# Expert sums of two prompt tiles as one dense pass over all rows of peer_v, in a fused decoder layer on one core

## The reference

```python
def peer(xn, w):                       # for each token
    ...
    s1 = jnp.einsum("thd,kd->thk", q[:, :, 0], w["peer_keys1"])     # 8 heads, 128 keys
    s2 = jnp.einsum("thd,kd->thk", q[:, :, 1], w["peer_keys2"])
    v1, i1 = lax.top_k(s1, PEER_TOPK)                               # 16
    v2, i2 = lax.top_k(s2, PEER_TOPK)
    ...
    top_s, sel = lax.top_k(cand, PEER_TOPK)                         # 16 of 256 pairs
    e = jnp.take_along_axis(cidx, sel, -1)                          # expert = 128 * key1 + key2
    gate = jax.nn.softmax(top_s.astype(F32), -1)
    act = jax.nn.gelu(jnp.einsum("td,thkd->thk", xb, w["peer_u"][e]).astype(F32), approximate=False)
    coef = (gate * act).astype(xb.dtype)
    return jnp.einsum("thk,thkd->td", coef, w["peer_v"][e])

h = h + peer(rmsnorm(h, w["norm_ffn"]), w)
gate = jax.nn.sigmoid((rmsnorm(h, w["norm_ple"]) @ w["w_ple_gate"]))
return h + gate * (p_i @ w["w_ple_proj"])
```

## Time and profile before

| | us |
|---|---|
| median of 3 runs | 4337.45 |
| lowest, highest | 4336.12, 4348.39 |
| span of the profiled execution | 4331.6 |
| TensorE busy (52%) | 2254.9 |
| VectorE busy (76%) | 3288.1 |
| ScalarE busy (12%) | 522.0 |
| GpSimd busy (51%) | 2201.2 |

### The profile page before, as it was taken

One profiled execution on the slowest core, in us unless ns is written; L12 is line 12 of the kernel. 1 busy time (PEld: TensorE's weight loads), 2 busy tenths in 40 slices (PEclk: granted clock), 3 DMA queues, 4 the chain that ended last, 5 costly groups with the idle time before them and its releaser, 6 DMA issues.

```text
span 4331.6 us, 24058 instructions
## 1 busy us (share of the span) xinstructions
PE 2254.9 (52%) x8238; PEld 1342.1 (31%) x8238; DVE 3288.1 (76%) x3700; ACT 522.0 (12%) x1098; POOL 2201.2 (51%) x1216
## 2 busy tenths in 40 slices
PE   8999815425899492779942457710000920000755
PEld 4456403213475131367731222710000410000322
DVE  0130699997667998868889856699999699988673
ACT  2220112122002001212212010000001000001001
POOL 0000365744332556468775653345667368877441
PEclk9999956657999796767865678955555965555877
DMA  8658789988997999989999899988989999999996
GB/s 294 250 223 287 303 357 364 422 323 335 424 423 299 422 424 414 353 356 365 406 374 360 347 400 413 405 345 339 399 365 405 424 415 422 422 407 422 424 408 234
DMA packets 261153, 1599.51 MB, mean 369 GB/s; under 512 B 27763, under 2 KB 49459, under 8 KB 91750
## 3 DMA queue, kind: packets, MB, share of 16 engines
q0 software_dynamic: 176064, 1268.30, 72.0%
q1 hardware_dynamic: 83078, 320.64, 19.5%
q10 hardware_dynamic: 1888, 9.03, 0.5%
HBM read 1554.75 MB, written 42.56 MB: 369 GB/s over the span
## 4 chain that ended last, share of the span: by engine, by line
PE 31%; DVE 30%; POOL 16%; DMA 13%; issue 7%; ACT 2%; SPq 0%; DVEq 0%; ACTq 0%; POOLq 0%
POOL ring L2549 16%; PE bank L826 14%; DVE ring L1968 11%; DVE total L1993 9%; DMA ring<-in_peer_v,idx_all 5%; DMA ring<-in_peer_u,idx_all 5%; PE bank L1251 4%; PE bank L1288 3%; PE bank L929 1%; PE bank L891 1%; PE bank L800 1%; PE bank L1079 1%; DMA front<-in_cache_kv_latent,page_rows 1%; DVE front L1744 1%; PE bank L1093 1%
## 5 line engine op out<-in xcount | busy, mean ns | idle before, releaser
L1993 DVE SCALAR_TENSOR_TENSOR total<-ring,gate_all,total 128x2048 f32<-128x2048 f32 x571 | 1341.8, 2350 | 188.0 <-DMA ring<-in_peer_v,idx_all 164.5
L2549 POOL DMA_INDIRECT ring<-in_peer_u,idx_all x576 | 1062.2, 1844 | 795.7 <-DVE total L1993 359.1
L2549 POOL DMA_INDIRECT ring<-in_peer_v,idx_all x576 | 1072.2, 1861 | 711.9 <-DVE total L1993 376.3
L1968 DVE CUSTOM_DVE_ANT_0 ring<-ring,xrow 128x2048 f32<-128x2048 f32 x576 | 1297.5, 2287 | 169.4 <-DMA ring<-in_peer_u,idx_all 167.5
L826 PE MATMUL bank<-front 128*128 128x512 f32 (+3 forms) x1920 | 838.3, 594 | 68.9 <-ACT front L2115 64.6
L800 PE MATMUL bank<-inv_diag,front 128*128 128x128 f32 (+1 forms) x304 | 61.9, 391 | 1159.3 <-DVE inv_diag L1378 1102.2
L826 PEld LDWEIGHTS bank<-front 128*128 128x128 f32 (+1 forms) x1920 | 338.4, 181 | 558.5 <-issue 554.5
L800 PEld LDWEIGHTS bank<-inv_diag,front 128*128 128x128 f32 (+1 forms) x304 | 58.9, 299 | 1164.2 <-DVE inv_diag L1378 1098.2
L1251 PE MATMUL bank<-front 128*128 128x128 f32 (+2 forms) x1536 | 257.0, 329 | 20.5 <-DMA front<-in_peer_w_q 17.4
L1251 PEld LDWEIGHTS bank<-front 128*128 128x128 f32 x1536 | 239.8, 192 | 39.3 <-DMA front<-in_peer_w_q 20.3
L2574 POOL DMA_DIRECT2D ring<-in_w_in x12 | 10.7, 894 | 342.8 <-PE bank L1288 239.6
(11 more groups left out here) (323 smaller groups left out, 2894.0 us busy)
## 6 DMA issues: line engine op xcount, KB each, us to landing
front<-in_w_in SPq DMA_DIRECT2D x64, 980.0 KB, 8.4
front<-in_w_out SPq DMA_DIRECT2D x48, 1024.0 KB, 9.1
front<-in_peer_w_q SPq DMA_DIRECT2D x48, 1024.0 KB, 13.3
front<-in_w_ple_gate SPq DMA_DIRECT2D x48, 1024.0 KB, 9.1
ring<-in_w_in POOLq DMA_DIRECT2D x12, 1960.0 KB, 10.5
front<-in_w_uq SPq DMA_DIRECT2D x6, 1536.0 KB, 10.7
ring<-in_peer_u,idx_all POOLq DMA_INDIRECT x576, 14.3
ring<-in_peer_v,idx_all POOLq DMA_INDIRECT x576, 16.0
```

The source lines that it names most:

```text
L1968: e.tensor_tensor_reduce(out=ring[:, b, :], in0=ring[:, b, :], in1=xrow[:, t % 2, :], scale=1.0, scalar=0.0, op0=ALU.mult, op1=ALU.add, ac ...
L1993: e.scalar_tensor_tensor(out=total, in0=ring[:, b, :], scalar=c1, in1=total, op0=ALU.mult, op1=ALU.add).then_inc(s("summed"), 1)
L2549: e.indirect_dma_start(out=ring[:, k % RING, :], out_offset=None, in_=a[("peer_u", "peer_v")[side]][0], in_offset=bass.IndirectOffsetOnAxi ...
```

## The change

Tiles 0, 1 and the sample (`SUMMED`) keep their sums. For tiles 2 and 3 (`DENSE`) only the dots are gathered. When a tile's gates are final, VectorE splits each pick's expert number into key 1 and key 2 (`spread`), TensorE turns both and the gates, and for each token VectorE makes two one-hot rows of 128x128, one with the gate in it; TensorE's product of the two is the token's 128 x 128 matrix of coefficients. ScalarE copies these into a stage and stores them to `c_dram` (16 MB for both tiles). When tile 3 is done too, the coefficients come back in the order of key 1, and TensorE multiplies, for each of 128 slabs of `peer_v` (all its rows, in order) and both tiles, 128x128 coefficients by 128x512 of the slab, 4 banks a tile: 1,024 products that add up in all 8 banks of PSUM. The sums are added to the residual rows, and the second embedding follows. The slots are 896 instead of 1,152.

```diff
+DENSE, SUMMED = [2, 3], [0, 1, 4]
+EB = 8
+GROUP = 4
+CHUNK = 16
...
 # VectorE
+            def spread(j):
+
+                t = DENSE[j]
...
+                e.wait_ge(s("gates_ready"), j + 1)
+                if j == 0:
+                    e.wait_ge(s("slabs_used"), PASSES["dense"])
+                mark(e.tensor_single_scalar(picks_u[:, j, 0, :], idx_all[:, row_units(t)], 7, ALU.logical_shift_right))
+                link(e.tensor_single_scalar(picks_u[:, j, 1, :], idx_all[:, row_units(t)], NKEY - 1, ALU.bitwise_and))
+                e.tensor_copy(picks[:, j, :, :], picks_u[:, j, :, :]).then_inc(s("picks_spread"), 1)
...
+                for q in range(G_GROUPS):
+                    n = j * G_GROUPS + q
+                    yield
+                    if n >= 2:
+                        e.wait_ge(s("g_psum"), n - 1)
+                    for i in range(GROUP):
+                        k = GROUP * q + i
+                        e.tensor_scalar(onehot[:, n % 2, 0, i, :], iota[:, :], picksT[:, j, 0, k:k + 1], picksT[:, j, 2, k:k + 1],
+                                        ALU.is_equal, ALU.mult)
+                        ins = e.tensor_scalar(onehot[:, n % 2, 1, i, :], iota[:, :], picksT[:, j, 1, k:k + 1], None, ALU.is_equal)
+                    ins.then_inc(s("picks_spread"), 1)
...
 # ScalarE
+                    if at == 0 and c >= 2:
+                        e.wait_ge(s(f"c_stored{c % 2}"), 16 * (c // 2))
+                    e.copy(stage[c % 2][:, :, at:at + GROUP].rearrange("p i n -> p n i"),
+                           bank[4 + n % 2][:, :].rearrange("p (n i) -> p n i", n=GROUP)).then_inc(s("g_staged"), 1)
+                    if at == CHUNK - GROUP:
+                        e.wait_ge(s("g_staged"), n + 1)
+                        e.dma_start(c_dram[c], stage[c % 2]).then_inc(s(f"c_stored{c % 2}"), 16)
...
+            def turned_coefficients():
+
+                half = EB // 2
+                for m in range(NKEY // half):
+                    b, i = m // 2, m % 2 * half
+                    yield
+                    e.wait_ge(s("pair_landed0"), 16 * (H_GLA // 2 + b + 1))
+                    if b:
+                        e.wait_ge(s("slabs_used"), PASSES["dense"] + EB * (b - 1) + i + half)
+                    e.copy(CT[:, i:i + half, :, :], CB[:, :, i:i + half, :].rearrange("p c i n -> p i c n")).then_inc(s("coefs_turned"), 1)
...
 # SyncE
+            embedding_loads(0)
+            expert_rows(0, 2)
+            coefficients(0)
+            expert_rows(2, SLABS + 2)
+            for b in range(1, NKEY // EB):
+                coefficients(b)
+                expert_rows(EB * (b - 1) + SLABS + 2, EB * b + SLABS + 2)
+            expert_rows(NKEY - EB + SLABS + 2, NKEY)
...
 # TensorE
+            def expert_sums():
+
+                e.wait_ge(s("g_staged"), G_GROUPS * len(DENSE))
+                for i in range(NKEY):
+                    n = PASSES["dense"] + i
+                    e.wait_ge(s(f"w_landed{n % SLABS}"), slab_landed(n))
+                    if i % (EB // 2) == 0:
+                        e.wait_ge(s("coefs_turned"), i // (EB // 2) + 1)
+                    for sl in range(len(DENSE)):
+                        cols = CT[:, i % EB, sl * P // CHUNK:(sl + 1) * P // CHUNK, :].rearrange("p c n -> p (c n)")
+                        for c in range(4):
+                            mm = e.matmul(bank[4 * sl + c][:, :], cols, W[:, n % SLABS, c * BANK:(c + 1) * BANK],
+                                          start=(i == 0), stop=(i == NKEY - 1))
+                    mm.then_inc(s("slabs_used"), 1)
+                e.wait_ge(s("v_added"), 4 * len(DENSE))
...
-PAGES_BEFORE = [395, 395, 395, 402, 404, 414, 414, 426, 428, 440, 440, 451, 452, 462, 467, 476]
+PAGES_BEFORE = [
+    267, 267, 267, 274, 274, 291, 291, 298, 298, 304, 304, 311, 311, 317, 317, 323]
```

More of the change, by code:

```diff
@@ L2440, in woven @@
                     yield from other_routes(g)
-                for pg in range(2):
-                    yield from embedding(pg)
+                yield from embedding(0)
+                for j in range(len(DENSE)):
+                    yield from spread(j)
+                yield from turned_coefficients()
+                yield from embedding(1)
             e.wait_ge(s("fills_ready"), 1)
```

247 lines of the change are left out of this document (174 added, 73 removed), and 65 rows, old and new, of the table ROWS_BEFORE.

## The result

| | us |
|---|---|
| before, median of 4 runs (lowest, highest) | 4336.78 (4334.12, 4348.39) |
| after, median of 4 runs (lowest, highest) | 4932.06 (4918.62, 4938.20) |
| ratio (95% interval) | 1.136 (1.134 to 1.138) |
| forecast (range) | 4742 (4560 to 4860) |

The page of the changed kernel: span, the engines' busy time, TensorE and DMA in 40 slices of 123 us. (PE is TensorE, PEld its weight loads, DVE VectorE, ACT ScalarE, POOL GpSimd.) The rows to hold against it are the earlier trace rows.

The account below looks back on a forecast made before the run. The kernel was taken as bound by DMA gathers and VectorE's slots, with TensorE holding a few stages. 3457 us to the end of tile 3's dots plus a 1279 us tail gave 4736 of span, 4742 us measured, range 4560 to 4860.

Parts of the forecast that it names:

- The price of a product: Dense pass: each fp32 product is two TensorE records, 0.87 us together; 1,024 products taken as 885 us.
- so the pass is TensorE's and not the DMA's: Dense pass: slabs need 152 GB/s, like slabs land in 9.1 us, four in flight, so TensorE's 885 us set it.
- rival D: Dense pass starves for slabs beside gathers: 52 us more if loads take 31 us; inside the main case, no separate chance.
- Ahead of the pass: From tile 3's last dot to the first product: spread 80 us, last store and first load 25, gates and transposes 10; 115.
- Behind the pass: From the last product to the end: 10 + 149 (second embedding) + 47 + 73 = 279 us.
- Up to T3: Until tile 3's dots end (T3): chain stages summing to 1843 us, then routing, slots, first embedding and tile 2's spread; 3457 us.
- The removed slots: 256 slots go, 224 of them before tile 3's last dot; claimed worth some 550 us, less than the added costs.
- The rule on VectorE and GpSimd's port: Tile 2's spread: 256 VectorE one-hots could lock GpSimd's port and hold back gathers, adding 0 to 51 us.
- A: Slots keep today's pace while the chain is carried: tile 3's dots end at 3306, the end 4591 us; chance 0.22.
- B: Stream held by DMA alone: tile 3's dots end at 2965, the end 4250 us, 2% faster; 0.05 together with E.
- E: Dense products cost one record each: 441 us less, 4300 us, faster; 0.05 together with B.
- C: More waits: spread throttled by stores (+100 us), no gain in first mixer stage (+112); 4840 to 4950 us; chance 0.13.

Follow-up runs that it names:

- e6: Changed kernel with two coefficient buffers, loads issued two batches ahead from ScalarE's queue, the first two batches chunk by chunk as stored: 4814.3 us, ratio 1.109.
- e2: Changed kernel with each coefficient load read as 128 contiguous pieces of 8 KB (wrong sums of tiles 2 and 3): 4801.0 us, ratio 1.107.
- e1: Changed kernel with the 16 coefficient loads issued from ScalarE's queue, leaving SyncE's queue to the value slabs: 4886.4 us, ratio 1.127.
- e4: Kernel before with the change's tables for the chain's steps, ScalarE and pages, all its own sums kept, no dense pass: 4639.4 us, ratio 1.070.
- e3: Changed kernel with the tables of the kernel before, each place moved down by the sums that are gone: 4841.6 us, ratio 1.116.

## Why the prediction was wrong

The time missed by 196 us of span: T3 came 107 us late, the pass took 97 more than forecast, the stretch ahead of it 21 more, and the one behind it 28 less, which hid a part. Two steps failed: the price of a missing slot in the stages up to T3, and the step by which the pass waits for nothing but TensorE. Step by step, in its order:

- **The price of a product** (0.43 us a record, 883 to 895 us): right for a pass that runs on; e6 has it at 881. In the change the stretches behind the waits ran at a granted clock of 0.94 to 0.97, which makes 894.
- **"so the pass is TensorE's and not the DMA's"**: this step failed. It looked at the slabs' bandwidth and at rival D's gathers, and they are indeed no limit (e2: no wait beside the same gathers). It left out the 16 coefficient loads between the slabs, although the change puts them in one queue with these: 88 us of waits, and the 12 us of slower products behind them. e1 removes the waits for slabs with the queue, e2 and e6 all waits of the pass, and e2 also shows that the piece size is what makes the load long. The text had named 512 B pieces for the first load only, and had the waits for slabs or coefficients among what would show it wrong.
- **Ahead of the pass** (115): 136. The first load was in a sum of about 25 us with the last store; by itself it took 44 (3654.3 to 3698.1), for the same reason. The spread was sized right by luck (87 us against 80), since it is held by something else: not by its stores, but by VectorE, 128 pairs of one-hots at 0.46 us (59 us) and nine slots.
- **Behind the pass** (279): 251. From the last product to the end of the second embedding it took 151 (10 + 149 by the forecast), from there to the sample's fold (L976, at 4859.1) 27 where 47 was taken from the earlier trace rows, and from there 73 as forecast. The 47 had held a wait of 27 us for in_p_sample and one of 10 for in_w_ple_proj beside the last gathers; here they are 8 and 6. TensorE's timeline before, then after:

```profile
4189.04 0.45 PE L862 MATMUL bank<-ident,front 64*128 64x64 f32 x2 [27.41 <-DMA front<-in_p_sample]
```

```profile
4840.23 0.44 PE L958 MATMUL bank<-ident,front 64*128 64x64 f32 x2 [7.75 <-DMA front<-in_p_sample]
```

- **Up to T3** (3457): 3564. This step failed too, by size. Every stage of the chain was sized with a price for a missing slot that came from VectorE's 2.33 us: 2.0 to 2.3 where it held the stage, 1.7 in the routing of group 1, 1.17 in the sample attention. The measured prices are 1.67 for 2.04 in the attention of group 1, 1.27 for 2.09 in that of tiles 3 and 4, and 0.71 for 1.17 in the sample attention, where TensorE is busy for 326 of the 364 us. So the stages sum to 1918 in place of 1843, +75: attention of group 1 370 for 350, attention of tiles 3 and 4 158 for 140, sample attention 364 for 340, the others within 8. The routing of tiles 3 and 4 took 121 for 101, since VectorE's own work in it is 116 and not the 101 that was left after taking 176 slots off. The stretch after it was right (113 slots 286 for 280; embedding 288 for 284; spread and 119 slots 373 for 375).
- **The removed slots** "are some 550 us": in the change's own tables 513 (e4 against the change), which is near. With the tables of before they are 279 (e3 against the kernel before). What the text never made a term of is the price of the tables: +303 us of T3 with all sums in place (e4), +68 without those of tiles 2 and 3 (e3 against the change). It was inside the stages, so the sum was not wrong by it, but a reader of it could not see that T3 moved by only 211 us in the end.
- **The rule on VectorE and GpSimd's port**: the stretch with the 256 one-hots of tile 2 took 373 us where the sum without the rule had 375. No cost of it shows, and GpSimd's timeline has the opposite: a gather's issue took 0.99 us beside the one-hots of tile 2, as where VectorE stood, and 1.9 to 2.2 us beside the dots.

```profile
3200.78 0.99 POOL L2743 DMA_INDIRECT ring<-in_peer_u,idx_all  x1 [4.85 <-DVE dots L2104]
...
3345.80 2.19 POOL L2743 DMA_INDIRECT ring<-in_peer_u,idx_all  x1 [0.30 <-issue]
```

- **Rivals.** A, B and E did not come: T3 came late and not early, and there are two records a product. C's range holds the time, but not its mechanisms: no throttling by stores, and the first mixer stage gained 92 us. D's place was right (slabs late in the pass) and its cause was not; it was also called harmless. The upper bound of the range, 4860, left no room for D with the coefficient loads in it.

## What to carry to other kernels

A load that stands in the same queue between others must be priced by its pieces: beside a full stream of 8 KB rows each piece waited about 0.3 us on its engine, so 1 MB in 2,048 pieces took 50 us and in 128 pieces 14. Another queue doesn't shorten it (65 us in e1), larger pieces do (e2), and an earlier issue hides it (e6). A slot that is removed gives what its stage had left, 0.7 us where TensorE holds and 2.5 where the DMA engines do: before work is taken out of a weave, measure that marginal price by moving the tables alone (e4). And work that replaces gathers by a dense pass has to lie beside other gathers: the last 510 us of the pass and the 250 behind it ran with none, at about 0.5 of the DMA share, and the tail cost more than the gathers that were saved.

## What the runs showed of the hardware

- The time of a 1 MB load beside the gathers rose with the number of its pieces, at the same bytes: 13.7, 30.8, 49.5 us for 128, 1,024, 2,048 pieces; 64.7 us for 2,048 with the slabs in another queue beside it, and 7.9 to 8.2 us with no gathers. Between the 2,048 pieces of 0.029 us stood 1,904 packets of 8 KB of 0.316 us.
- A product of 128x128 by 128x512 in fp32 is two records of 0.43 us at a granted clock of 1.00 (2,048 in 881 us), and 0.45 in the stretch behind a wait of 27 us (128 in 57.75 us, clock 0.95); in bfloat16, read as every second half-word of fp32 data, it is one record of 0.25 to 0.32 us (8 in 1.98, 32 in 10.1 us).
- ScalarE's copy of 128x512 from PSUM took 1.02 to 1.07 us into the stage, whose elements lie apart, against 0.605 for the nearest copy of the kernel before. That the spacing is the reason was not tested.
- A gather's issue on GpSimd took 0.99 us beside VectorE's 128x128 one-hots and 1.9 to 2.2 us beside its dots.
